# The expert layer's second product: 128 prompt tokens leave it, their chosen rows of V are fetched by number

## The reference

```
v1, i1 = lax.top_k(s1, PEER_TOPK)
v2, i2 = lax.top_k(s2, PEER_TOPK)
cand = (v1[..., :, None] + v2[..., None, :]).reshape(..., PEER_TOPK * PEER_TOPK)
sc, pos = lax.top_k(cand, PEER_TOPK)
e = jnp.take_along_axis(cidx, pos, axis=-1)
gate = jax.nn.softmax(sc, axis=-1)
u = jnp.take(u_tab, e, axis=0)
act = jax.nn.gelu(jnp.einsum('tpkd,td->tpk', u, hb), approximate=False)
vv = jnp.take(v_tab, e, axis=0)
return jnp.einsum('tpk,tpkd->td', gate * act, vv)
```

## Time and profile before

| | |
|---|---|
| median of 3 runs | 2484.13 us |
| profiled execution | 2486.54 us, span 2484.8 us |
| TensorE matmuls busy | 2303.5 us (93%) |
| VectorE busy | 1728.3 us (70%) |
| GpSimd busy | 894.6 us (36%) |
| ScalarE busy | 868.5 us (35%) |
| DMA | 339.18 MB, mean 137 GB/s |

### The profile page before, as it was taken

The page is one execution under the profiler, slowest core; times in us unless marked ns, Lnnn a source line. Parts: engine busy times, 40 slices in busy tenths (PEclk is TensorE's granted clock), DMA queues, the critical chain, the costliest instruction groups (busy, mean ns, idle before and its releaser), DMA issues.

```text
span 2484.8 us, 49280 instructions
## 1 busy us (share of the span) xinstructions
PE 2303.5 (93%) x18541; PEld 2239.9 (90%) x18541; DVE 1728.3 (70%) x2736; ACT 868.5 (35%) x1375; POOL 894.6 (36%) x352
## 2 busy tenths in 40 slices
PE   5999987888999999599999999998999999999997
PEld 5988877877889999599999999998999999999997
DVE  6444446336788989869999999944666666666665
ACT  4443333232334434234444444433222222222221
POOL 2222223223324344233333333335445354443531
PEclk9999988988999999799999999999999999999998
DMA  5232220311223433234444444457555655556540
GB/s 194 87 98 86 78 83 21 106 38 51 89 72 123 137 130 129 75 120 171 171 162 167 171 161 168 164 184 238 182 188 170 191 173 175 186 174 195 166 148 36
DMA packets 168557, 339.18 MB, mean 137 GB/s; under 512 B 10512, under 2 KB 84400, under 8 KB 166192
## 3 DMA queue, kind: packets, MB, share of 16 engines
q1 hardware_dynamic: 168496, 338.46, 40.8%
HBM read 260.04 MB, written 78.38 MB: 136 GB/s over the span
## 4 chain that ended last, share of the span: by engine, by line
PE 49%; issue 31%; POOL 13%; DVE 3%; ACT 2%; DMA 1%; POOLq 0%; DVEq 0%; SPq 0%; ACTq 0%
PE bank L730 14%; PE bank L728 14%; PE bank L729 14%; POOL u_lo L640 12%; PE bank L790 1%; PE bank L997 1%; DVE mixedT L1599 1%; PE bank L781 1%; PE bank L1025 1%; DVE rmo L1721 1%; PE bank L835 1%; DMA g<-scratch_gates 0%; DVE rms L1589 0%; PE bank L804 0%; POOL h_lo L656 0%
## 5 line engine op out<-in xcount | busy, mean ns | idle before, releaser
L728 PE MATMUL bank<-h_hi,u_hi 128*128 128x272 f32 x3136 | 925.9, 295 | 83.4 <-POOL u_lo L640 32.5
L730 PE MATMUL bank<-h_hi,u_lo 128*128 128x272 f32 x3136 | 914.1, 291 | 0.0
L729 PE MATMUL bank<-h_lo,u_hi 128*128 128x272 f32 x3136 | 909.3, 290 | 0.0
L640 POOL TENSOR_TENSOR u_lo<-wring,u_hi 128x1024 fp32r<-128x1024 f32 x196 | 521.7, 2662 | 1066.1 <-ACT u_hi L1443 665.4
L728 PEld LDWEIGHTS bank<-h_hi,u_hi 128*128 128x128 f32 x3136 | 598.5, 191 | 96.4 <-issue 61.8
L729 PEld LDWEIGHTS bank<-h_lo,u_hi 128*128 128x128 f32 x3136 | 598.6, 191 | 0.5
L730 PEld LDWEIGHTS bank<-h_hi,u_lo 128*128 128x128 f32 x3136 | 596.7, 190 | 0.0
L728 PE MATMUL bank<-w_hi,v_hi 128*128 128x272 f32 x2048 | 587.5, 287 | 6.2 <-DVE xT L1897 4.5
L730 PE MATMUL bank<-w_hi,v_lo 128*128 128x272 f32 x2048 | 593.1, 290 | 0.0
L729 PE MATMUL bank<-w_lo,v_hi 128*128 128x272 f32 x2048 | 591.5, 289 | 0.0
L640 POOL TENSOR_TENSOR v_lo<-wring,v_hi 128x1024 fp32r<-128x1024 f32 x128 | 341.1, 2698 | 410.0 <-ACT v_hi L1525 410.0
(11 more groups left out here) (223 smaller groups left out, 1981.1 us busy)
## 6 DMA issues: line engine op xcount, KB each, us to landing
wring<-in_u SPq DMA_DIRECT2D x128, 512.0 KB, 3.7
wring<-in_v SPq DMA_DIRECT2D x128, 512.0 KB, 3.3
scratch_act<-actb SPq DMA_DIRECT2D x128, 272.0 KB, 2.1
scratch_gates<-gst SPq DMA_DIRECT2D x17, 2048.0 KB, 7.3
a<-scratch_act SPq DMA_DIRECT2D x32, 1088.0 KB, 6.4
g<-scratch_gates SPq DMA_DIRECT2D x32, 1088.0 KB, 9.5
wring<-in_w_in SPq DMA_DIRECT2D x28, 512.0 KB, 3.9
wring<-in_w_x SPq DMA_DIRECT2D x24, 512.0 KB, 4.1
```

What stands on the lines that cost most here:

```text
L640: pool.tensor_tensor(dst, wring[:, slot], hi.bitcast(F32), ALU.subtract).then_inc(lo_ready, 1)
L728: pe.matmul(out, whi, xhi, start=first, stop=False)
L729: pe.matmul(out, whi, xlo, start=False, stop=False)
L730: return pe.matmul(out, wlo, xhi, start=False, stop=last)
```

## The change

The first 128 prompt tokens (RARE) leave the dense second product. The other 416 stay: one matmul of 416 columns for each key, bank and pass, and each of the 8 banks gathers its sum over all 128 keys before VectorE adds it to `xT` once. The halves of V and of the weights stand in rings of four keys, given back by `v_used`. V's low half is made by VectorE (L1982), not by GpSimd.

For the 128 tokens that left, tokens stand on partitions. VectorE computes the row number of each chosen expert (`place_v`) and the place of its activation (`place_a`). GpSimd fetches by indirect DMA: for each of the 128 choices r, one row of V for each token (`rows_v`, 4 buffers) and one activation for each token (`pick_act`). VectorE multiplies activations and gates (`pick_w`) and adds weight times row to `y_s`, one choice for about each key from key 10 on. At the end TensorE transposes `y_s` in 8 blocks, and VectorE adds them to `xT`.

The gate stage handles 13 chunks (the 416 tokens), so 17 groups of the first product stand ahead of it, 13 in it and 2 behind it. Its comparisons and products have all operands in bf16, with tokens in pairs in the last dimension (key, 2) in place of a key dimension over which one value is broadcast. The third ranking looks at 100 candidates instead of 256: the 3 best of the first half with all 16, and the other 13 with the best 4; six small operations per tile turn positions in that list into ranks.

```diff
-NCHUNK = T // CTOK
+RARE = P
+DENSE = T - RARE
+NCHUNK = DENSE // CTOK
+PICKS = PH * TOPK
+VRING, ROWS = 4, 4
+FIRST_PICK = 10
...
+WHOLE, NARROW = 3, 4
+NCAND = WHOLE * TOPK + (TOPK - WHOLE) * NARROW
...
-            with pool.Fori(0, KEYS // GROUP // 2) as i:
-                for p in range(2):
-                    for j in range(GROUP):
-                        low(i * 8 + (FRONT + NPQ + KEYS + 4 * p + j), j,
-                            vs[p][1][:, j].rearrange("p (c n) -> p c n", c=C),
-                            vs[p][0][:, j].rearrange("p (c n) -> p c n", c=C))
+            def expert_row(r):
+                if r >= ROWS:
+                    pool.wait_ge(pick_added, r - ROWS + 2)
+                pool.indirect_dma_start(rows_v[:, r % ROWS], None, experts,
+                                        bass.IndirectOffsetOnAxis(place_v[:, r:r + 1], 0)
+                                        ).then_inc(row_landed[r % ROWS], 16)
+
+            def activation_of(r):
+                pool.indirect_dma_start(pick_act[:, r:r + 1], None, acts,
+                                        bass.IndirectOffsetOnAxis(place_a[:, r:r + 1], 0)).then_inc(pick_landed[r // TOPK % 2], 16)
+
+            pool.wait_ge(picked, 1)
+            pool.wait_ge(unit_done, 4 + 2 * (NPQ + KEYS))
+            for j in range(GROUP):
+                pool.wait_ge(act_stored[j], 16 + 16 * (KEYS // GROUP))
+            for r in range(TOPK):
+                activation_of(r)
+            for r in range(PICKS):
+                expert_row(r)
+                if r + TOPK < PICKS:
+                    activation_of(r + TOPK)
...
-                    for n in range(2 * C):
-                        b, h = n // 2, n % 2
-                        pe.wait_ge(y_taken, (i * 2 + p) * (2 * C) + (n + 1))
-                        for j in range(GROUP):
-                            m = passes(bank[n % 8][:, 0:HT], vs[p][0][:, j, b * P:(b + 1) * P],
-                                       vs[p][1][:, j, b * P:(b + 1) * P], wbs[p][0][:, j, half(h)],
-                                       wbs[p][1][:, j, half(h)], j == 0, j == GROUP - 1)
+            def second_products(k, j, first, last):
+
+                pe.wait_ge(lo_ready, k + (FRONT + NPQ + KEYS + 1))
+                pe.wait_ge(w_ready, k + 1)
+                for b in range(C):
+                    m = passes(bank[b][:, 0:DENSE], v_hi[:, j, b], v_lo[:, j, b], w_hi[:, j], w_lo[:, j], first, last)
+                    if last:
                         m.then_inc(y_ready, 1)
+                    elif b == C - 1:
+                        m.then_inc(v_used, 1)
...
+            pe.wait_ge(pick_added, PICKS + 1)
+            for b in range(C):
+                pe.wait_ge(y_taken, b + 1)
+                pe.transpose(bank[b][:, 0:P], y_s[:, b * P:(b + 1) * P], ident[:]).then_inc(yt_ready, 1)
...
-                    step.link(dve.tensor_tensor(hot1[:, j % 2], every, spread(0), ALU.is_equal))
+                    step.link(dve.tensor_tensor(hot1[:, j % 2], keys, spread(chosen[:, 0, tok]), ALU.is_equal))
...
-                        a = dve.tensor_tensor(gated[:, j % 2, q], hot1[:, j % 2],
-                                              pieces[:, q, tok][:, :, None].to_broadcast([P, TOK8, KEYS]), ALU.mult)
+                        a = dve.tensor_tensor(gated[:, j % 2, q], hot1[:, j % 2], spread(pieces[:, q, tok]),
+                                              ALU.mult)
...
+            def add_pick(r):
...
+                if r % TOPK == 0:
+                    these = slice(r, r + TOPK)
+                    dve.wait_ge(pick_landed[r // TOPK % 2], 16 * TOPK * (r // TOPK // 2 + 1))
+                    step.link(dve.tensor_tensor(pick_w[:, these], pick_act[:, these], sel[:, 0, 2, these], ALU.mult))
+                dve.wait_ge(row_landed[r % ROWS], 16 * (r // ROWS + 1))
+                dve.wait_ge(pick_added, r + 1)
+                dve.scalar_tensor_tensor(out=y_s[:], in0=rows_v[:, r % ROWS], scalar=pick_w[:, r:r + 1], in1=y_s[:],
+                                         op0=ALU.mult, op1=ALU.add).then_inc(pick_added, 1)
...
+            for k in range(GROUP, KEYS):
+                product_gates(k)
+                value_low(k)
+                due = PICKS * max(0, k + 1 - FIRST_PICK) // (KEYS - FIRST_PICK)
+                while added < due:
+                    add_pick(added)
+                    added += 1
+                weight_low(k)
+            for b in range(C):
+                dve.wait_ge(y_ready, b + 1)
+                x = xT[:, b, RARE:T]
+                dve.tensor_tensor(x, bank[b][:, 0:DENSE], x, ALU.add).then_inc(y_taken, 1)
+            for b in range(C):
+                dve.wait_ge(yt_ready, b + 1)
+                x = xT[:, b, 0:RARE]
+                dve.tensor_tensor(x, bank[b][:, 0:P], x, ALU.add).then_inc(x_final, 1)
+                if b:
+                    add_squares(C * NORM_FINAL + b - 1, T, (b - 1) % 2)
```

More of the change, by code:

```diff
@@ L212, in encoder_step @@
         ag_landed = [sem("ag_landed0"), sem("ag_landed1")]
-        w_ready, y_ready, y_taken = sem("w_ready"), sem("y_ready"), sem("y_taken")
+        w_ready, v_used = sem("w_ready"), sem("v_used")
+        row_landed = [sem(f"row_landed{q}") for q in range(ROWS)]
+        picked, pick_added = sem("picked"), sem("pick_added")
+        pick_landed = [sem("pick_landed0"), sem("pick_landed1")]
+        y_ready, y_taken, yt_ready, x_final = sem("y_ready"), sem("y_taken"), sem("yt_ready"), sem("x_final")
         halves = Plan(nc, plan.end)
@@ L1867, in _ @@
                 dve.wait_ge(sel_ready, t + 1)
+            place_f, row = rankf[:, 0], gsum[:, 0:1]
+            step.link(dve.tensor_tensor_reduce(out=place_f, in0=ident[:], in1=iota[:], scale=1.0, scalar=0.0,
+                                               op0=ALU.mult, op1=ALU.add, accum_out=row))
+            step.link(dve.scalar_tensor_tensor(out=place_f, in0=sel[:, 0, 0], scalar=float(KEYS), in1=sel[:, 0, 1],
+                                               op0=ALU.mult, op1=ALU.add))
+            step.link(dve.tensor_copy(place_v[:], place_f))
+            step.link(dve.tensor_scalar(place_f, place_f, float(T), row, ALU.mult, ALU.add))
+            dve.tensor_copy(place_a[:], place_f).then_inc(picked, 1)
             dve.wait_ge(selT_taken, 1)
@@ L1874, in _ @@
                     step.link(dve.tensor_tensor(selT[:, 2], selT[:, 2], pieces[:, q], ALU.subtract))
+            dve.tensor_copy(chosen[:], selT[:, 0:2])
+            step.link(dve.tensor_copy(every[:], iota[:][:, :, None].to_broadcast([P, KEYS, 2])))
             with dve.Fori(0, NCHUNK) as i:
@@ new lines, in spread @@
+                    def spread(row):
+                        pairs_of = row.rearrange("p (a b) -> p a b", b=2)
+                        return pairs_of[:, :, None, :].to_broadcast([P, TOK8 // 2, KEYS, 2])
+                    keys = every[:][:, None].to_broadcast([P, TOK8 // 2, KEYS, 2])
+                    step.link(dve.tensor_tensor(hot1[:, j % 2], keys, spread(chosen[:, 0, tok]), ALU.is_equal))
+                    dve.tensor_tensor(hot2[:, j % 2], keys, spread(chosen[:, 1, tok]), ALU.is_equal)
@@ L1930, in _ @@
-            pairs = KEYS // GROUP // 2
-            weighted(0, 0, 32, lambda units: None)
-            weighted(1, 1, 32, lambda units: add_products(0, units))
-            with dve.Fori(0, pairs - 1) as i:
-                weighted(i * 2 + 2, 0, (i + 2) * 32, lambda units: add_products(i * 2 + 1, units))
-                weighted(i * 2 + 3, 1, (i + 2) * 32, lambda units: add_products(i * 2 + 2, units))
-            add_products(2 * pairs - 1, range(2 * C), last=True)
-            dve.wait_ge(y_taken, 8 + 16 * 2 * pairs)
+            vb = FRONT + NPQ + KEYS
@@ new lines, in _ @@
+            step.restart()
+            product_gates(0)
+            for k in range(1, GROUP):
+                product_gates(k)
+                weight_low(k - 1)
+            weight_low(GROUP - 1)
+            for k in range(GROUP):
+                value_low(k)
+            added = 0
+            for k in range(GROUP, KEYS):
+                product_gates(k)
+                value_low(k)
+                due = PICKS * max(0, k + 1 - FIRST_PICK) // (KEYS - FIRST_PICK)
[3 more added lines that the diff above has]
+                weight_low(k)
@@ L1938, in _ @@
+            add_squares(C * NORM_FINAL + C - 1, T, (C - 1) % 2)
             normed(NORM_FINAL, xT, yT, T)
```

185 lines of the change are left out of this document (94 added, 91 removed).

## The result

The changed kernel took 2219.24 us (2216.26 to 2220.2, 4 runs) against 2484.18 before: ratio 0.8933, 95% interval 0.8918 to 0.8948. The sum was made against the profiled execution of before, and its counterpart took 2218.4 us (span 2216.6) where the sum said 2183.5. So 268 us were won where 303 were forecast, 35 fewer.

The account below looks back on a forecast made before the run. TensorE was taken as the bound nearly everywhere, with VectorE close in the gate stage. From the median 2484.1 us, terms of -225, -28, -32, -26 and +8 gave 2181 us; range 2150 to 2310.

Parts of the forecast that it names:

- rival A: Whole kernel: the forecast itself, TensorE stays the bound everywhere, 2150 to 2215 us; chance 0.60.
- B: Last stage: matmuls of 416 columns carry the excess, 185.2 to 191.5 ns, total 2215 to 2235 us; chance 0.11.
- C: Last stage: gathers or DMA set the pace, 2279 us at 2.5 us per gather, 2226 at 320 GB/s; chance 0.20.
- Matmuls of 416 columns: Last stage on TensorE: 3072 matmuls bound by columns, 174 ns each, 534.5 us; 125 ns read as a floor.
- The stage's start and DMA: Last stage: 7 us for stalls at its start and 10 us for DMA bursts, added to the matmul time.
- GpSimd and VectorE: Last stage: gathers take 1 to 1.5 us and stay hidden; VectorE needs 3.78 of 4.18 us per key.
- D: Last stage: gathers on GpSimd shut out VectorE's two-input operations, slower than before, 2620 us at 1.8 us per gather; chance 0.08.
- The stall before the gates: TensorE's idle 26.8 us near 1018 goes, through VectorE's shorter ranking and 96 us more cover: -28 us.
- The gate stage: 16 units lose their gates, -32 us; bf16 pairs remove TensorE's 0.5 us wait in 52 units, -26 us.
- The tail: After the last product: additions of 416 columns, then of 128 with sums of squares behind them: +8 us.

Follow-up runs that it names:

- two kernels with the burst: The changed kernel with all 256 candidates in the third ranking, 2216.6 us; the changed kernel with its gathers' burst begun after 8 keys, 2214.7 us.

## Why the prediction came out as it did

The direction and the stated range were right. The sum was 35 us too low: one term was 44 too low, and 9 were given back by others (7 ahead of the second product, 2 at its start). 2219 lies outside the 2150 to 2215 of the forecast, rival A, so the range held because it was drawn to take in B and C, not because A came true.

*Matmuls of 416 columns.* This step failed: 3072 x 174 should have been 3072 x 188.4, 44 us more. The reasoning was that an excess added to each matmul "would show" at the half clock, so that 125 ns had to be a floor. The half-clock rows were right (346 to 347 ns for 416, nothing over), the conclusion was not: the excess exists only at the full clock. Of the 15.1 ns at 416 columns, 2.6 are there in every variant, some 8 come with operands read at a step of 4 bytes (6.9 with the moving one alone), 4.4 with fp32r. The result fell into rival B, for which I had 0.11; its bounds 185.2 and 191.5 held the value. The Trainium skill's rule (TensorE: Matmul & The Clock Gate, "Wait — 56ns, not 53.3ns?") holds to 0.1 ns for bf16 side by side (175.9 ns against 175.8), and misses fp32r by 12.6 ns.

*The stage's start and DMA.* 7 + 10 us charged, 15 found, but not where I put them: DMA at a share of 0.96 slows nothing, and without picks the stage runs without any gap. The 15 us go with the gathers' burst.

*GpSimd and VectorE (rivals C and D).* A gather takes 0.94 to 1.05 us, starts 1.25 us apart: my lower side, 1 to 1.5. VectorE's low half stayed at 1226 ns with a maximum of 1227. The collision exists, the other way round: 55 of the 256 gathers took 1.3 us or more, up to 1.95, and every one of them started while an operation of VectorE with two inputs ran. Both rivals' conditions were thus absent.

*The stall before the gates.* All of it went, as forecast, but the reason was the cover, not the ranking: with 256 candidates the changed kernel is as fast, and pruning alone gives 17 us. "VectorE is thus some 35 us sooner" was wrong: in the pruned kernel alone the rankings end 33 us sooner, but the exponential comes only 13 sooner (1027.3 against 1040.6). The decoding's small operations cost 7 us as charged (8); the 14 us of stretched operations were put at nothing.

*The gate stage.* VectorE's operations took the 0.69 us of the sum (where it says "halves the elements per ns", "doubles" is meant). The unit went from (1636.6 - 1096.9)/67 = 8.06 us to (1547.0 - 1164.0)/51 = 7.51: 28 us for 52 units (26 forecast), and 16 x (8.06 - 48 x 0.1257) = 32 (32). The pair layout costs TensorE 1.8 ns per gate matmul (58.0 against 56.2), 2 us in all, where I charged nothing. With the stall's 28 this makes 88 of the 93 us; 1 of the rest is the shorter pause ahead of the second product (0.8 us between two starts, 1.9 before), the others are not traced.

*The tail.* +8, as forecast.

## What to carry to other kernels

A distance between matmuls that is longer than its columns is to be measured at two widths and at the clock that will be granted before it is scaled; one clock says nothing of the other. A stretch where an engine stands at "issue" just after many small DMAs were asked for in a row is worth a try at pacing them: here it gave 16 us for two waits. One profiled execution may be the lucky one: two kernels with the burst showed 1.7 and 2.5 us of gaps in theirs, while all their other runs were 9 to 15 us longer. And a stall may vanish by cover alone; test each of its cures by itself before keeping the costlier one.

## What the runs showed of the hardware that I had not expected

- At the full clock, TensorE's distance depends on the step at which the moving operand is read: 175.9 ns for 416 bf16 columns side by side, 182.8 to 184.0 at 4 bytes, 188.4 in fp32r; at the half clock 416 fp32r columns take 346 to 347, which is 416/1.2.
- 208 fp32r columns took 111.3 ns, 14 more than the line through 272 and 416 columns gives; no narrower one was tried.
- At 416 columns the weights' step and count hardly matter: 64 columns of weights instead of 128 save 0.9 ns.
- Indirect DMAs on GpSimd (128 rows of 4096 bytes, or 128 of 4) take much the same to issue, 1.05 and 0.94 us as a median; those that start beside a two-input operation of VectorE take up to 1.95.
- Some 20 of them in a row, 1.25 us apart, can cost TensorE 15 us of gaps, and sometimes cost 2.
- At 337 GB/s and a DMA share of 0.96, matmuls run as at 212 GB/s.
